# A recurrent layer whose first convolution tap, norm sum and order of roots are moved between engines

## What is computed

```python
def rglru_mixer(x, w_in, conv_w, conv_b, gate_w, gate_b, a_param, w_out):
    y_br, x_br = jnp.split(x @ w_in, 2, axis=-1)        # 1024 -> 2 x 1280
    y_br = jax.nn.gelu(y_br)
    xc = causal_dwconv(x_br, conv_w, conv_b)            # 4 taps
    g = jnp.einsum('bsnc,gncd->gbsnd', xb, gate_w)      # 10 blocks of 128, two gates
    g = jax.nn.sigmoid(g + gate_b)
    log_a = -8 * r_gate * jax.nn.softplus(-a_param)
    a = jnp.exp(log_a)
    bterm = jnp.sqrt(-jnp.expm1(2.0 * log_a)) * i_gate * xc
    h = scan(a, bterm)                                  # h[t] = a[t] h[t-1] + b[t]
    return (h * y_br) @ w_out
h = x + rglru_mixer(rmsnorm(x, lru_norm_g), ...)        # rmsnorm: x * rsqrt(mean(x^2) + eps) * g
```

## Time and profile before

| | |
|---|---|
| median of 3 runs | 2144.28 us (2134.29 to 2150.36) |
| profiled execution | 2143.21 us, of which the span is 2141.3 us |
| TensorE busy | 2024.0 us (95% of the span), mean granted clock 0.969 |
| VectorE busy | 1521.3 us (71%) |
| ScalarE busy | 876.9 us (41%) |
| recurrent layer | to about 136 us of the span |

### The profile page before, as it was taken

How to read it: one execution, slowest core, us unless ns; L and a number is a source line. 1 busy time by engine, 2 the same in 40 slices (tenths; PEclk the granted TensorE clock), 3 DMA queues, 4 the chain that set the end, 5 groups by cost and what they waited for, 6 DMA issues and landing times.

```text
span 2141.3 us, 34007 instructions
## 1 busy us (share of the span) xinstructions
PE 2024.0 (95%) x13036; PEld 1777.3 (83%) x13036; DVE 1521.3 (71%) x2771; ACT 876.9 (41%) x1386; POOL 377.9 (18%) x354
## 2 busy tenths in 40 slices
PE   7899999978999999988999999999998998999998
PEld 6789999857999888745888878888887865999998
DVE  6668888686888659865887658575666956675554
ACT  4634344254444522277343332212214336554443
POOL 0003334002233700001100122301240000004223
PEclk9999999979999999999999999999998999999999
DMA  6345565603545522201444325454553310544552
GB/s 233 135 173 183 195 236 207 216 1 137 196 178 215 188 99 79 79 1 40 162 172 167 130 71 193 157 197 177 196 216 131 116 60 1 190 176 167 190 191 92
DMA packets 46991, 318.14 MB, mean 149 GB/s; under 512 B 5008, under 2 KB 8080, under 8 KB 9488
## 3 DMA queue, kind: packets, MB, share of 16 engines
q1 hardware_dynamic: 45568, 309.58, 39.7%
q0 software_dynamic: 1296, 6.82, 0.9%
HBM read 315.33 MB, written 1.05 MB: 148 GB/s over the span
## 4 chain that ended last, share of the span: by engine, by line
PE 71%; DVE 19%; ACT 5%; issue 4%; DVEq 1%; DMA 0%; POOL 0%; ACTq 0%; POOLq 0%
PE ps L661 68%; DVE w_lo L1548 7%; ACT arena L1153 3%; PE ps L906 2%; DVE arena L1705 1%; DVE arena L1703 1%; DVE small L1747 1%; DVE ps L1701 1%; DVE arena L1767 1%; DVE ps L1714 1%; DVE ps L1736 1%; DVE arena L1920 1%; ACT w_hi L1153 1%; ACT L1153 1%; DVE arena L1655 1%
## 5 line engine op out<-in xcount | busy, mean ns | idle before, releaser
L661 PE MATMUL ps<-h_hi,w_hi 128*128 128x256 f32 (+1 forms) x2616 | 836.5, 320 | 32.0 <-DVE h_lo L1535 12.4
L661 PE MATMUL ps<-h_lo,w_hi 128*128 128x256 f32 (+1 forms) x2616 | 825.1, 315 | 0.0
L661 PE MATMUL ps<-h_hi,w_lo 128*128 128x256 f32 (+1 forms) x2616 | 824.8, 315 | 0.0
L1548 DVE TENSOR_TENSOR w_lo<-ring,w_hi 128x1024 fp32r<-128x1024 f32 x457 | 579.9, 1276 | 324.6 <-ACT w_hi L1153 323.2
L1153 ACT ACTIVATE w_hi<-ring 128x1024 fp32r<-128x1024 f32 x457 | 475.2, 1054 | 531.0 <-PE ps L661 482.4
L661 PEld LDWEIGHTS ps<-h_hi,w_hi 128*128 128x128 f32 x2616 | 498.2, 190 | 75.1 <-issue 19.7
L661 PEld LDWEIGHTS ps<-h_lo,w_hi 128*128 128x128 f32 x2616 | 498.7, 191 | 33.2
L661 PEld LDWEIGHTS ps<-h_hi,w_lo 128*128 128x128 f32 x2616 | 498.2, 190 | 33.3
L1153 ACT ACTIVATE arena<-ps 128x512 f32<-128x512 f32 (+2 forms) x246 | 140.9, 575 | 376.5 <-PE ps L661 327.9
L661 PE MATMUL ps<-hid_hi,w_hi 128*128 128x256 f32 (+1 forms) x736 | 223.8, 304 | 1.1 <-DVE w_lo L1548 1.0
L1569 DVE SCALAR_TENSOR_TENSOR ps<-ring,arena 128x512 f32<-128x512 f32 x320 | 223.7, 768 | 0.0
(11 more groups left out here) (193 smaller groups left out, 2045.3 us busy)
## 6 DMA issues: line engine op xcount, KB each, us to landing
ring<-wstream SPq DMA_DIRECT2D x290, 1024.0 KB, 4.8
arena<-c_in POOLq DMA_DIRECT2D x7, 512.0 KB, 4.6
arena<-rpb POOLq DMA_DIRECT2D x2, 1536.0 KB, 6.7
x<-x_in SPq DMA_DIRECT2D x2, 1024.0 KB, 12.2
out<-arena SPq DMA_DIRECT2D x8, 128.0 KB, 2.1
cst<-consts SPq DMA_DIRECT2D x1, 928.0 KB, 12.2
prm<-params SPq DMA_DIRECT2D x1, 580.0 KB, 10.8
ring<-wstream SPq DMA_DIRECT2D x1, 512.0 KB, 3.5
```

The lines of the kernel that those rows point to most:

```text
L661: ins = nc.tensor.matmul(*a, **k)
L1548: V.tensor_tensor(w_lo[:, job % SPLITS, :], raw_job(job), w_hi[:, job % SPLITS, :].bitcast(F32), ALU.subtract).then_inc(weights_ready, 1)
```

## The change

- The sum of squares of the first norm: ScalarE squares all eight tiles into eight slots, with no wait between; VectorE adds them up (seven additions); TensorE does one product with the ones in place of eight.
- ScalarE does a square root of a constant before the input lands. It rounds job 0 behind the squares, ahead of the root, and jobs 1 and 2 between the copies of the norm's tiles (behind the fourth and the sixth), where all three stood ahead of the root.
- VectorE does rest job 0 behind the sums, rest job 1 ahead of the last `h_lo`, rest job 2 behind it. The scaling of a parameter (`q_g`) and the first two small operations on `a_param` move from ahead of the norm's tiles to behind rest job 2; the wait for the parameters now stands ahead of the first scaling.
- The first tap of tiles 0 to 9, with its bias, is formed by ScalarE from the bank (Identity with scale and bias), announced by `first_tap`; VectorE waits for that and adds the three others.
- The Exp of the decay moves on ScalarE to just ahead of tile 10, and the row of small operations on VectorE to behind the taps of tile 9 and rest jobs 13 and 14.
- Square roots 0 to 7, then the gelus of tiles 16 to 19, then square roots 8 and 9. VectorE does the root's arguments 0 to 7, recurrences 0 and 1, arguments 8 and 9, recurrences 2 to 9; the last four wait for the gelus of tiles 16 to 19.

```diff
--- before.py
+++ after.py
@@ -437,6 +437,7 @@
         ctx_squared, ctx_mean, ctx_root, ctx_root_ready = (sem(n) for n in ("ctx_squared", "ctx_mean", "ctx_root", "ctx_root_ready"))
         ctx_gain_ready, ctx_scaled, ctx_full, ctx_h_ready = (sem(n) for n in ("ctx_gain_ready", "ctx_scaled", "ctx_full", "ctx_h_ready"))
         squares_summed, mean_ready = sem("squares_summed"), sem("mean_ready")
+        x_summed, x_mean, first_tap = sem("x_summed"), sem("x_mean"), sem("first_tap")
         gate_scaled, token_roots, root_inverted = sem("gate_scaled"), sem("token_roots"), sem("root_inverted")
         scaled_ready, h_ready = sem("scaled_ready"), sem("h_ready")
         act_tile_ready = sem("act_tile_ready")
@@ -702,13 +703,6 @@
             def free(stage, b, n):
 
                 pe.wait_ge(acc_free[b], n + USED[stage][b])
-
-            def norm(N):
-                for k in range(KD):
-                    pe.wait_ge(squares_ready, squares.next())
-                    ins = nc.tensor.matmul(psO[:, 0:N], ones[:], sq[:, k % 4, 0:N], start=k == 0, stop=k == KD - 1)
-                    if k:
-                        ins.then_inc(sums_ready, 1)
 
             def token_root(N, terms, spread):
 
@@ -910,7 +904,9 @@
             pe.wait_ge(ones_ready, 1)
 
 
-            norm(S)
+            squares.next(KD)
+            pe.wait_ge(x_summed, 1)
+            mm(psO[:, 0:S], ones[:], scaled[:, 0, :], start=True, stop=True).then_inc(x_mean, 1)
             gate_w = raw("lru_gate")
 
             def lru_gates(a, b):
@@ -1157,24 +1153,6 @@
                 act.wait_ge(*summed)
                 go(rs[0:rows, 0:N], bank[0:rows, 0:N], ACT.Sqrt, scale=1.0 / width, bias=eps[0:rows, :]).then_inc(root_ready, 1)
 
-            def norm(N, ready, middle=None):
-                for k in range(KD):
-                    ready(k)
-                    if k >= 4:
-                        act.wait_ge(sums_ready, sums.base + max(k - 4, 1))
-                    go(sq[:, k % 4, 0:N], x[:, k, 0:N], ACT.Square).then_inc(squares_ready, 1)
-                sums.base += KD - 1
-                if middle:
-                    middle()
-                root_of(N, psO, D, (sums_ready, sums.base))
-
-            def h_norm(N, ready, middle=None):
-
-                norm(N, ready, middle)
-                for k in range(KD):
-                    act.wait_ge(scaled_ready, scaled_c.next())
-                    go(h_at[S][0][:, k, 0:S], scaled[:, k % 8, :], ACT.Copy).then_inc(h_rounded, 1)
-
             def token_squares(N, ready):
 
                 go(tok[:, 8:9], eps[:], ACT.Sqrt)
@@ -1209,11 +1187,18 @@
                 go(o, i, func, **k).then_inc(acc_free[b], 1)
 
             act.wait_ge(ones_ready, 1)
+            go(tok[:, 8:9], eps[:], ACT.Sqrt)
             act.wait_ge(x_landed, 16)
-            h_norm(S, lambda k: None, middle=lambda: start_run("lru_in"))
+            for k in range(KD):
+                go(scaled[:, k, :], x[:, k, 0:S], ACT.Square).then_inc(squares_ready, 1)
+            round_job(0, 0)
+            root_of(S, psO, D, (x_mean, 1))
+            for k in range(KD):
+                act.wait_ge(scaled_ready, scaled_c.next())
+                go(h_at[S][0][:, k, 0:S], scaled[:, k, :], ACT.Copy).then_inc(h_rounded, 1)
+                if k in (3, 5):
+                    round_job((k - 1) // 2, 0)
             act.wait_ge(params_landed, 16)
-            act.wait_ge(dve_tile_ready, tiles.next())
-            go(sca[:, 0:10], sca[:, 0:10], ACT.Exp).then_inc(act_tile_ready, 1)
             def lru_y(j):
 
                 copy("lru_in", j % 4, j // 4, l_y[:, j - KL, :], acc[j % 4][:, 0:S], func=ACT.Gelu_apprx_tanh)
@@ -1226,8 +1211,15 @@
                 go(l_i[:, n, :], acc[b][:, S:S2], ACT.Sigmoid, bias=par("gate_b", KL + n)).then_inc(acc_free[b], 1)
 
             for j in range(16):
+                if j == KL:
+                    act.wait_ge(dve_tile_ready, tiles.next())
+                    go(sca[:, 0:10], sca[:, 0:10], ACT.Exp).then_inc(act_tile_ready, 1)
                 ahead("lru_in", j)
-                if j >= KL:
+                if j < KL:
+                    full("lru_in", j % 4, j // 4)
+                    go(l_x[:, j, :], acc[j % 4][:, 0:S], ACT.Identity, scale=par("lru_cw", j * CONV_L + CONV_L - 1),
+                       bias=par("lru_cb", j)).then_inc(first_tap, 1)
+                else:
                     lru_y(j)
             for n in range(4):
                 lru_sigmoid(n)
@@ -1240,9 +1232,10 @@
             for n in range(KL):
                 go(l_b[:, n, :], l_r[:, n, :], ACT.Exp, scale=sca[:, 20 + n:21 + n])
                 go(l_t[:, n, :], l_r[:, n, :], ACT.Tanh, scale=sca[:, 30 + n:31 + n]).then_inc(act_tile_ready, 1)
-            for j in range(16, 20):
-                lru_y(j)
             for n in range(KL):
+                if n == KL - 2:
+                    for j in range(16, 20):
+                        lru_y(j)
                 act.wait_ge(dve_tile_ready, tiles.next())
                 go(l_t[:, n, :], l_t[:, n, :], ACT.Sqrt).then_inc(act_tile_ready, 1)
 
@@ -1538,11 +1531,6 @@
                         mid()
                 hn.base += len(tiles)
 
-            def h_norm(N, gain):
-
-                inverse(N)
-                h_tiles([(k, 0) for k in range(KD)], gain, rs, h_at[S])
-
             def rest_job(job, turn):
                 dve.wait_ge(weights_rounded, turn * (SLOTS * HALF // JOB) + (job + 1))
                 V.tensor_tensor(w_lo[:, job % SPLITS, :], raw_job(job), w_hi[:, job % SPLITS, :].bitcast(F32),
@@ -1622,15 +1610,35 @@
 
             V.memset(eps[:], EPS)
             V.memset(ones[:], 1.0).then_inc(ones_ready, 1)
-            start_run("lru_in")
+            for k in range(1, KD):
+                dve.wait_ge(squares_ready, k + 1)
+                ins = V.tensor_tensor(scaled[:, 0, :], scaled[:, 0, :], scaled[:, k, :], ALU.add)
+                if k < KD - 1:
+                    link(ins)
+            ins.then_inc(x_summed, 1)
+            rest_job(0, 0)
+            inverse(S)
             dve.wait_ge(params_landed, 16)
-            dve.wait_ge(x_landed, 16)
+            h_tiles([(k, 0) for k in range(KD)], lambda k, s: par("lru_g", k), rs, h_at[S], mid=lambda: rest_job(1, 0))
+            rest_job(2, 0)
             link(V.tensor_scalar(par("q_g", 0, 2), par("q_g", 0, 2), DH ** -0.5, None, ALU.mult))
 
             a_, e_, z_, z2_, s_ = par("a_param", 0, KL), sca[:, 0:10], sca[:, 10:20], sca[:, 20:30], sca[:, 30:40]
             link(V.tensor_scalar(e_, a_, -1.0, None, ALU.mult))
             V.tensor_tensor(e_, e_, a_, ALU.min).then_inc(dve_tile_ready, 1)
-            h_norm(S, lambda k, s: par("lru_g", k))
+            for t in range(KL):
+                ahead("lru_in", t)
+                dve.wait_ge(first_tap, t + 1)
+                o, i = l_x[:, t, :], acc[t % 4][:, 0:S]
+                for d in range(1, CONV_L):
+                    ins = V.scalar_tensor_tensor(out=o[:, d:], in0=i[:, 0:S - d], scalar=par("lru_cw", t * CONV_L + CONV_L - 1 - d),
+                                                 in1=o[:, d:], op0=ALU.mult, op1=ALU.add)
+                    if d < CONV_L - 1:
+                        link(ins)
+                    else:
+                        ins.then_inc(acc_free[t % 4], 1)
+            for j in range(KL, KL + 2):
+                ahead("lru_in", j)
             dve.wait_ge(act_tile_ready, at.next())
             link(V.tensor_scalar(z2_, e_, 2.0, None, ALU.add))
             link(V.reciprocal(z2_, z2_))
@@ -1646,32 +1654,37 @@
             link(V.tensor_scalar(sca[:, 20:30], e_, -8.0, None, ALU.mult))
             V.tensor_scalar(sca[:, 30:40], e_, 8.0, None, ALU.mult).then_inc(decay_ready, 1)
 
-            for t in range(KL):
-                ahead("lru_in", t)
-                full("lru_in", t % 4, t // 4)
-                o, i = l_x[:, t, :], acc[t % 4][:, 0:S]
-                link(V.tensor_scalar(o, i, par("lru_cw", t * CONV_L + CONV_L - 1), par("lru_cb", t), ALU.mult, ALU.add))
-                for d in range(1, CONV_L):
-                    ins = V.scalar_tensor_tensor(out=o[:, d:], in0=i[:, 0:S - d], scalar=par("lru_cw", t * CONV_L + CONV_L - 1 - d),
-                                                 in1=o[:, d:], op0=ALU.mult, op1=ALU.add)
-                    if d < CONV_L - 1:
-                        link(ins)
-                    else:
-                        ins.then_inc(acc_free[t % 4], 1)
-            for j in range(KL, 17):
+            for j in range(KL + 2, 17):
                 ahead("lru_in", j)
 
-            for n in range(KL):
-                dve.wait_ge(act_tile_ready, at.next())
+            turned = at.base
+
+            def decay_square(n):
+
+                dve.wait_ge(act_tile_ready, turned + n + 1)
                 link(V.tensor_tensor(l_r[:, n, :], l_b[:, n, :], l_b[:, n, :], ALU.mult))
                 V.scalar_tensor_tensor(out=l_t[:, n, :], in0=l_r[:, n, :], scalar=1.0, in1=l_t[:, n, :],
```

(18 more changed lines are left out.)

## The result

| | before | after |
|---|---|---|
| median of 7 runs | 2148.48 us (2134.29 to 2150.36) | 2133.72 us (2130.57 to 2139.95) |
| span of the profiled execution | 2141.3 us | 2129.9 us |
| first add of `lru_out`'s result to `x` | 135.58 us | 126.78 us |

The ratio of the times is 0.9944, with a 95% interval of 0.9922 to 0.9967: a real gain, within 1% (12 us, 7 to 17). The layer's end moved by 8.8 us, against 8.7 forecast.

A forecast was written before the change was run, and what follows sets the result against it. Bound by stretch: serial norm chain, VectorE in `lru_in` tiles, later TensorE and ScalarE. Gates 7.5 us earlier, first recurrence 10.1, less 1.4 for the bank: 8.7 off 2143.2 gives 2134.5 us; range 2125 to 2144.

The forecast's parts named there:

- Before the first product: First norm, from input to first scaling: shorter sum and earlier table load start scaling at 14.25 us, 5.3 us earlier.
- Scaling and tile 0: First scaling to end of tile 0: added rest job and roundings leave 3.9 of the 5.3 us gained.
- T0: End of tile 0 of `lru_in` on TensorE: forecast at 22.2 us, against 26.1 before.
- Tiles 1 to 11: `lru_in` tiles: VectorE drops from 3.14 to 2.57 us, TensorE paces at 2.77; gates at 52.7, 7.5 us gained.
- SP's late half: Weights of jobs 18 and 19, loaded after rest job 15, land some 5 us later: no cost, up to 1 us.
- Gates to the first recurrence: Gates through roots: all moves by 7.5 us, one load before the first root; first recurrence at 90.9, 10.1 us earlier.
- The bank's wait: Start of `lru_out`: TensorE does one product, then waits for a gelu to free its bank until 92.7, costing 1.4 us.
- The clock: Idle gap before `lru_out`: granted clock falls to half speed as before, at the same price of 2.8 us.
- Rival 2: Gap before `lru_out` too short for the clock to fall: 11.5 us gained, 2132 us; chance 0.15.
- The sum: Whole kernel: 8.7 us off the profiled execution's 2143.2 gives 2134.5 us; forecast's chance 0.55.

The follow-up runs named there:

- Runs 1 to 6: Changed kernel with tap, decay operations, both undone; kernel before with tap, decay operations moved; tap undone, rest job 15 earlier: gates 52.56, 56.76, 58.73, 56.85, 56.21, 52.59 us.
- filling products: Changed kernel with gelus behind the second root, plus seven unused fp32 products on TensorE between tile 19 and `lru_out`: first add 122.53 us, ratio to before 0.9937.
- both back: Changed kernel with the first tap on VectorE and the decay operations ahead of the tiles again: gates 58.73 us, first add 131.69 us.

## Why the prediction was right, step by step

- **Before the first product** (5.3 us forecast, scaling at 14.25): 5.1, at 14.43. The additions ran from 7.58 to 10.77 (10.8 forecast) and the root began at 12.13 (11.9). The parameters held nothing up.
- **Scaling and tile 0** (T0 = 22.2, 3.9 us left): the tap of tile 0 is at 22.34, and the norm's return made the gates 4.0 later.
- **Tiles 1 to 11** (gates at 52.7): 52.07 and 53.28 in two executions, at 2.72 and 2.83 us a tile, where the prediction had 2.73 to 2.80. The sum was right; the reason was only half so. The prediction credited the 0.57 us that VectorE loses per tile. It named the row of small operations as without cover, but priced only the row's new place, at nothing. Runs 1 to 6 show that in the kernel before either edit takes the tiles to TensorE's pace, and that in the changed kernel it is the row's move that does it: 4.7 us at the gates, and the tap none.
- **SP's late half** ("no cost, and up to 1 us if late"): no wait in the kernel after; with the tap back it is 1.3 and 2.45 us, of which 1.0 reaches TensorE. This was the tight place, and what the tap pays for.
- **Gates to the first recurrence**: the load ahead of the roots at 87.13 (87.2), first recurrence done at 90.9 (90.9). Here two misses cancel. The gates moved by 8.1 us, not 7.5, and 0.5 us was lost again to a fall of the clock at the second gates, which the prediction did not have. That part of the agreement is luck.
- **The bank's wait**: forecast to 92.7, seen at 92.73. The order of the roots is worth 0.8 net, not 1.2 (the 0.4 is the clock's); moving the gelus to the second root takes the wait away, and 0.7 to 1.2 us with it (two executions of each). The Trainium skill, ScalarE: Activation LUTs, section "What ACT_TABLE_LOAD costs", adds a drain of 1380 ns to a load. Here the eighth root ends at 90.98, the second load takes 91.00 to 92.28 and its gelu begins at 92.29, so this trace shows no drain.
- **The clock**: it fell as taken, from 91.3 to 98.1, with 6.0 us of `lru_out`'s products in it, 5.4 of them behind the wait for the gelu. Rival 2 did not come, and the filling products show that its price, 2.8, was about right (2.4 and 2.9 us against the two executions without them).
- **The sum**: 8.7 forecast, 8.8 at the first add. 2134.5 us forecast, 2133.7 measured. That the medians meet within 1 us is luck: the forecast was taken off an execution of 2143.2, while the kernel before had a median of 2148.5 in the comparison, and the medians' gain, 14.8 us, is more than the 7.3 to 11.5 that the prediction allowed. The range rested on the scatter of the runs, and had to.

## What to carry to other kernels

When a producer with 3.14 us a tile feeds a consumer with 2.7, a lead of a few microseconds at the start is worth as much as a faster producer over nine tiles, and the two gains are not to be added; ask which is left when the other is there. Work without cover at the start of such a series is the first thing to move. Work that is moved past a queue's release pays there: look at what frees the next transfer before calling the move free. When executions scatter by more than an edit is worth, compare marks in the trace near the edit, and look at where the granted clock was low in each trace before a cause is named.

## What the runs showed of the hardware

- At a granted clock of 1.00 the same products (128x256, fp32 rounded) run at one of two paces, 24 in 2.72 or in 2.83 us (the gaps between ScalarE's taps, 30.51 to 33.23 in the kernel after and 30.91 to 33.73 in the first with early gelus). It holds over eleven tiles, and differs between executions of one program. That is 1.25 us in 11 tiles, and the kernel has some 10,000 products of rounded operands, so it alone could make most of the scatter of the runs. The traces bear this out in part: behind the layer's first add, where all programs are the same, the shortest trace (both back, 1998.0 us) has the fastest mean pace, 113.9 ns, and the two longest (norm back, 2009.5; filling products, 2012.3) the slowest, 115.2; between them the order is mixed, for the low clock counts too. Where it changes, it may change back at the next stretch: in both executions of the kernel after, tiles 1 to 11 and tiles 12 to 15 have opposite paces.
- A single wait of 2.9 us on TensorE cost 4.6, because the clock was low for 3.4 us, from 1.2 us behind the wait's end.
- The same wait of 2.6 us ahead of the second gates left the clock up in four traces, at half speed for 3.4 us in six and for 6.8 us in two. From the gates to the load ahead of the roots it was 34.5 us in the four, 34.6 to 35.1 in the six and 36.4 in the two. Two executions of one program differed in this.
- Seven unused products (3.2 us) in a gap of 4 us went with a clock that stayed up and gave 2.4 us back on the work behind, in one execution; in the 13 traces without them the clock fell there each time.
